# Sums spread between tiles, feed-forward results pair by pair, the hybrid output projection as split products

## What is computed

```python
def swiglu(x, w_in, w_out):
    gate, up = jnp.split(x @ w_in, 2, axis=-1)
    return (jax.nn.silu(gate) * up) @ w_out
...
def sb_rwkv_mixer(hn, w_in, w_out, mu, w0, w2, a0, a2, g2, k_k, k_a, r_k, ln_w, ln_b):
...
    o_a = stick_breaking_attention(hd(qa), hd(ka), hd(va)).reshape(b, s, SB_WIDTH)
    o_b = rwkv7_time_mix(rw, mu, w0, w2, a0, a2, g2, k_k, k_a, r_k, ln_w, ln_b)
    return jnp.concatenate([o_a, o_b.astype(o_a.dtype)], axis=-1) @ w_out
...
        h = h + mix
        h = h + conv_glu(rmsnorm(h, ffn_norm[i]), ffn_w_in[i], ffn_conv_w[i], ffn_conv_b[i], ffn_w_out[i])
        e = rmsnorm(p[i] @ ple_w_proj[i], ple_norm[i])
        gate = jax.nn.sigmoid(rmsnorm(h, ple_gate_norm[i]) @ ple_w_gate[i])
        h = h + gate * e
```

## Time and profile before

| | |
|---|---|
| time, median of 3 runs | 1332.56 us (1331.33 to 1334.46) |
| time of the profiled execution | 1332.49 us |
| its span, first to last instruction | 1330.8 us |
| PE busy | 1305.4 us, 98% |
| DVE busy | 932.6 us, 70% |
| ACT busy | 650.8 us, 49% |
| mean granted PE clock, of the full one | 0.994 |
| fp32 output product of `hyb` (L1136) | 128 records in 28.1 us |

### The profile page before, as it was taken

How to read it: one execution, slowest core, us unless ns; L and a number is a source line. 1 busy time by engine, 2 the same in 40 slices (tenths; PEclk the granted TensorE clock), 3 DMA queues, 4 the chain that set the end, 5 groups by cost and what they waited for, 6 DMA issues and landing times.

```text
span 1330.8 us, 27655 instructions
## 1 busy us (share of the span) xinstructions
PE 1305.4 (98%) x11856; PEld 1261.9 (95%) x11856; DVE 932.6 (70%) x1232; ACT 650.8 (49%) x759; POOL 96.3 (7%) x103
## 2 busy tenths in 40 slices
PE   9999999999999999999999999999999899999998
PEld 8999999998999999999989889999999779999997
DVE  6766666696567666778774457777787776977676
ACT  6444444474345444555624434444375575444445
POOL 0000000141000000003020100000000160000000
PEclk9999999999999999989999999999999999999999
DMA  9555565543355555533420055555544404555540
GB/s 365 192 196 202 201 209 191 190 141 115 133 191 200 204 190 190 189 132 135 169 96 4 1 178 193 199 189 192 199 160 142 158 1 163 197 204 195 189 158 33
DMA packets 34912, 219.16 MB, mean 165 GB/s; under 512 B 4411, under 2 KB 6884, under 8 KB 9612
## 3 DMA queue, kind: packets, MB, share of 16 engines
q1 hardware_dynamic: 32032, 215.62, 45.9%
q10 hardware_dynamic: 2796, 2.31, 0.5%
HBM read 216.72 MB, written 1.06 MB: 164 GB/s over the span
## 4 chain that ended last, share of the span: by engine, by line
PE 92%; DVE 4%; issue 1%; ACT 1%; DMA 1%; POOL 0%; SPq 0%; POOLq 0%; ACTq 0%; DVEq 0%
PE ps L957 47%; PE ps L1003 17%; PE ps L1136 2%; PE ps L920 2%; PE ps L1118 2%; PE ps L900 2%; PE ps L1634 2%; PE ps L1083 2%; PE ps L1281 2%; PE ps L926 1%; PE ps L1676 1%; PE ps L1707 1%; PE ps L1465 1%; DVE arena L2983 1%; PE ps L1474 1%
## 5 line engine op out<-in xcount | busy, mean ns | idle before, releaser
L2604 DVE TENSOR_TENSOR weights_second_parts<-weight_bays,weights_first_parts 128x2048 fp32r<-128x2048 f32 x130 | 296.4, 2288 | 123.5 <-ACT weights_first_parts L1834 123.4
L1834 ACT ACTIVATE weights_first_parts<-weight_bays 128x2048 fp32r<-128x2048 f32 x130 | 248.4, 1914 | 216.4 <-PE ps L957 177.0
L957 PE MATMUL ps<-x_first_part,weights_first_parts 128*128 128x256 f32 x1472 | 195.6, 276 | 0.0
L957 PE MATMUL ps<-x_first_part,weights_second_parts 128*128 128x256 f32 x1472 | 194.5, 275 | 0.0
L957 PE MATMUL ps<-x_second_part,weights_first_parts 128*128 128x256 f32 x1472 | 194.4, 275 | 0.0
L957 PEld LDWEIGHTS ps<-x_first_part,weights_first_parts 128*128 128x128 f32 x1472 | 179.1, 192 | 0.6 <-issue 0.6
L957 PEld LDWEIGHTS ps<-x_first_part,weights_second_parts 128*128 128x128 f32 x1472 | 179.1, 192 | 0.2 <-DVE weights_second_parts L2604 0.2
L957 PEld LDWEIGHTS ps<-x_second_part,weights_first_parts 128*128 128x128 f32 x1472 | 179.2, 192 | 0.0
L1003 PE MATMUL ps<-hidden_first_part,weights_first_parts 128*128 128x256 f32 x704 | 136.3, 275 | 0.0
L1003 PE MATMUL ps<-hidden_second_part,weights_first_parts 128*128 128x256 f32 x704 | 131.5, 275 | 0.0
L1003 PE MATMUL ps<-hidden_first_part,weights_second_parts 128*128 128x256 f32 x704 | 131.5, 275 | 0.0
(11 more groups left out here) (478 smaller groups left out, 2334.2 us busy)
## 6 DMA issues: line engine op xcount, KB each, us to landing
weight_bays<-in_conv_in SPq DMA_DIRECT2D x44, 1024.0 KB, 4.7
weight_bays<-in_ffn_in SPq DMA_DIRECT2D x42, 1024.0 KB, 4.8
weight_bays<-in_ffn_out SPq DMA_DIRECT2D x22, 1024.0 KB, 4.8
weight_bays<-in_conv_out SPq DMA_DIRECT2D x22, 1024.0 KB, 4.8
weight_bays<-in_mix_in SPq DMA_DIRECT2D x19, 1024.0 KB, 4.9
weight_bays<-in_hyb_in SPq DMA_DIRECT2D x13, 1024.0 KB, 4.9
weight_bays<-in_ple_gate SPq DMA_DIRECT2D x12, 1024.0 KB, 4.7
weight_bays<-in_mix_out SPq DMA_DIRECT2D x4, 1024.0 KB, 5.0
```

Of the source, the lines that this page charges most:

```text
L957: mm = nc.tensor.matmul(dst, w[:, k, j * P:j * P + width], x[:, k], start=(n + k == 0), stop=(n == 2 and k == KD - 1))
L1834: nc.scalar.activation(hi, raw, ACT.Copy).then_inc(*w_hi_ready.inc(f, g, kind, of - g))
L2604: v.tensor_tensor(lo, raw, hi, ALU.subtract).then_inc(*w_lo_d.inc(f, g, kind, of - g))
```

## The change

It has three parts, and some that follow from them.

- The sums of squares for the norm behind a `ple` stage are no longer made in one piece at the head of the next stage. Pair 0 is added inside `ple`, ahead of the last gate tile, pairs 1 and 2 at the head of the next stage, pair 3 behind the `embed` of pair 0. In `mix1`, `embed` of pair 1 moves behind the sums. In a `ple` stage DVE adds all four pairs to `h` before it makes second parts of x. DVE's second part of `mix1`'s chunk 1 is made ahead of the norm's factors.
- In a feed-forward's last group the three products are made for two tiles at a time, so that pairs are complete one after another.
- The output product of `hyb` is made of 192 products of split parts in place of 64 products of float32 values. ACT and DVE split its four chunks of weights, the attention outputs (DVE's part of pairs 0 and 1 between levels of the recurrence's inverse) and the recurrence's outputs. `turn_y` moves into the middle of chunk 1.

```diff
@@ -550,7 +550,16 @@
         ysq, _ = carve(at - 3072, 2, 8, 64)
-        oaT = xT[:, 0:4]
+        oa_hi, oa_lo = mixer_hi[:, 0:4], mixer_hi[:, 4:8]
+        ob_hi, _ = carve_split(20480, "recurrent_outputs_first_part", 4, SEQ)
+        ob_lo, _ = carve_split(21504, "recurrent_outputs_second_part", 4, SEQ)
+        hyb_out_hi = [carve_split(n * BAY, f"hybrid_out_first_parts_{n}", BAY)[0] for n in range(4)]
+        def hyb_out_views(n):
+            c = chunks["hyb_out", n] % BAYS
+            return bay[:, c], hyb_out_hi[n][:], bay_lo[:, c]
@@ -870,15 +879,24 @@
-            def add_weighted_squares(n, b):
-                for k in range(KD):
-                    if k % 2 == 0:
-                        pe.wait_ge(*squared.at(n, k // 2))
+            def add_weighted_pair(q, b):
+                for k in (2 * q, 2 * q + 1):
                     for t in range(TT):
                         mm = nc.tensor.matmul(ps[:, b, 2 * t:2 * t + 2], sq[:, k, t * P:(t + 1) * P], gain_pairs[:, k],
                                               start=(k + t == 0), stop=(k == KD - 1), skip_group_check=True)
-                mm.then_inc(*sums_p.inc(n))
+                return mm
+            def add_squares_behind(stage, q):
+                n = key_after(stage)
+                pe.wait_ge(*squared.at(n, q))
+                if n == "hyb":
+                    mm = add_weighted_pair(q, 4)
+                else:
+                    mm = add_pair(sq, q, 4)
+                if q == PAIRS - 1:
+                    mm.then_inc(*sums_p.inc(n))
@@ -1017,14 +1035,16 @@
                         wait_split(pe, (w_lo_d,), f, "out", g, i)
-                        for tile in range(KD):
-                            add(tile, 0, hi, hid_hi)
-                            add(tile, 1, lo, hid_hi)
-                        wait_hidden(pe, hid_lo_ready, f, g, i)
-                        for tile in range(KD):
-                            mm = add(tile, 2, hi, hid_lo)
-                            if tile in (1, 3, 5):
-                                mm.then_inc(*acc_ready.inc(f, tile // 2))
+                        for q in range(PAIRS):
+                            for tile in (2 * q, 2 * q + 1):
+                                add(tile, 0, hi, hid_hi)
+                                add(tile, 1, lo, hid_hi)
+                            if q == 0:
+                                wait_hidden(pe, hid_lo_ready, f, g, i)
+                            for tile in (2 * q, 2 * q + 1):
+                                mm = add(tile, 2, hi, hid_lo)
+                            if q < PAIRS - 1:
+                                mm.then_inc(*acc_ready.inc(f, q))
@@ -1123,33 +1143,16 @@
-            def project_rows(name, srcT, key, at_chunk={}):
...
             def whole_x(n):
                 for q in range(PAIRS):
                     pe.wait_ge(*x_d.at(n, q))
             def mix1():
                 pe.wait_ge(consts_in.sem, 16 * N_CONSTS)
-                embed("ple1", 0, 4, (0, 1))
+                embed("ple1", 0, 4, (0,))
                 add_first_pairs("mix1", 0)
                 add_last_pair("mix1", 0)
-                embed("ple1", 0, 4, (2,))
+                embed("ple1", 0, 4, (1, 2))
@@ -1301,6 +1304,10 @@
                             pe.wait_ge(*ple_d.at(stage, 1))
+                            if stage == "ple1":
+                                pe.wait_ge(*cols_ready.at("block"))
+                            if stage != "ple21":
+                                add_squares_behind(stage, 0)
@@ -1319,12 +1326,13 @@
             def hyb():
-                pe.wait_ge(*rb_ready.at("ple1"))
-                pe.wait_ge(*cols_ready.at("block"))
-                add_weighted_squares("hyb", 4)
-                embed("ple20", 1, 0, (0, 1))
+                add_squares_behind("ple1", 1)
+                add_squares_behind("ple1", 2)
+                embed("ple20", 1, 0, (0,))
+                add_squares_behind("ple1", 3)
+                embed("ple20", 1, 0, (1, 2))
                 spread("hyb", 6, 2)
-                embed("ple20", 1, 0, (2, 3))
+                embed("ple20", 1, 0, (3,))
...
@@ -1598,15 +1606,27 @@
-                def first_rwkv_part():
-                    turn_y()
-                    pe.wait_ge(*sol_d.at("ob", 0))
-                def second_rwkv_part():
-                    pe.wait_ge(*sol_d.at("ob", 1))
-                pe.wait_ge(*stick_a.at("out", 3))
-                project_rows("hyb_out", lambda k: oaT[:, k] if k < 4 else obT[:, k - 4], "hyb", at_chunk={2: first_rwkv_part, 3: second_rwkv_part})
+                for n in range(4):
+                    hi, lo = (t.rearrange("p (a b) -> p a b", a=2) for t in hyb_out_views(n)[1:])
+                    first, second, at = (oa_hi, oa_lo, 2 * n) if n < 2 else (ob_hi, ob_lo, 2 * n - 4)
+                    pe.wait_ge(*w_hi_ready.at("hyb_out", n))
+                    pe.wait_ge(*w_lo_d.at("hyb_out", n))
+                    if n == 0:
+                        pe.wait_ge(*stick_d.at("out", 3))
+                    if n >= 2:
+                        pe.wait_ge(*sol_a.at("ob", n - 2))
+                        pe.wait_ge(*sol_d.at("ob rest", n - 2))
+                    for tile in range(KD):
+                        if (n, tile) == (1, 4):
+                            turn_y()
+                        dst = ps[:, tile // 2, tile % 2 * SEQ:(tile % 2 + 1) * SEQ]
+                        for m, (w, x) in enumerate(((hi, first), (lo, first), (hi, second))):
+                            for j in range(2):
+                                mm = nc.tensor.matmul(dst, w[:, j, tile * P:(tile + 1) * P], in_halves(x[:, at + j]), start=(n + j + m + tile % 2 == 0),
+                                                      stop=(n == 3 and j == 1 and m == 2), skip_group_check=True)
+                        if n == 3 and tile in (1, 3, 5):
+                            mm.then_inc(*acc_ready.inc("hyb", tile // 2))
+                    through(mm, ("hyb_out", n))
...
@@ -2153,7 +2172,7 @@
                     act.wait_ge(*stick_p.at("out", g))
-                    nc.scalar.activation(oaT[:, g], ps[:, STICK_BANK[g], 0:256], ACT.Copy).then_inc(*stick_a.inc("out", g))
+                    nc.scalar.activation(oa_hi[:, g], ps[:, STICK_BANK[g], 0:256], ACT.Copy).then_inc(*stick_a.inc("out", g))
@@ -2201,11 +2220,24 @@
                 stick_weights(3)
+                def first_parts_of_rows(n):
+                    raw, hi, _ = hyb_out_views(n)
+                    wait_weights(act, ("hyb_out", n))
+                    act.wait_ge(*sol_p.at("y", n // 2))
+                    nc.scalar.activation(hi, raw, ACT.Copy).then_inc(*w_hi_ready.inc("hyb_out", n))
                 keep_unknowns(1)
                 stick_keep(2)
+                first_parts_of_rows(0)
+                first_parts_of_rows(1)
                 stick_keep(3)
                 keep_outputs(1)
                 squares_of_outputs(1)
+                first_parts_of_rows(2)
+                first_parts_of_rows(3)
+                for n in range(2):
+                    act.wait_ge(*sol_d.at("ob", n))
+                    nc.scalar.activation(ob_hi[:, 2 * n:2 * n + 2], obT[:, 2 * n:2 * n + 2], ACT.Copy).then_inc(*sol_a.inc("ob", n))
@@ -2505,13 +2537,10 @@
                     update(q, h[:, 2 * q:2 * q + 2]).then_inc(*h_ready.inc(n, q))
-                    if n.startswith("ple"):
-                        if q == 1:
-                            second_parts(n, 0, gain)
-                    elif gain and q:
+                    if gain and q and not n.startswith("ple"):
                         second_parts(n, q - 1, gain)
                 if n.startswith("ple"):
-                    for q in range(1, PAIRS):
+                    for q in range(PAIRS):
...
@@ -3001,13 +3030,24 @@
+                def stick_rest(g):
+                    dve.wait_ge(*stick_a.at("out", g))
+                    v.tensor_tensor(oa_lo[:, g], ps[:, STICK_BANK[g], 0:256], oa_hi[:, g], ALU.subtract).then_inc(*stick_d.inc("out", g))
+                def rest_of_rows(n):
+                    raw, hi, lo = hyb_out_views(n)
+                    dve.wait_ge(*w_hi_ready.at("hyb_out", n))
+                    v.tensor_tensor(lo, raw, hi, ALU.subtract).then_inc(*w_lo_d.inc("hyb_out", n))
                 level(0)
                 stick_softplus(0)
                 level(1)
                 stick_softplus(1)
                 level(2)
                 level(3)
+                stick_rest(0)
                 level(4)
+                stick_rest(1)
@@ -3041,7 +3081,12 @@
                 normed(0)
+                stick_rest(2)
+                rest_of_rows(0)
+                rest_of_rows(1)
+                stick_rest(3)
                 normed(1)
+                rest_of_rows(2)
@@ -3050,6 +3095,11 @@
                     v.tensor_tensor(part, part, ps[:, 6 + n].rearrange("p (a s) -> p a s", a=2), ALU.mult).then_inc(*sol_d.inc("ob", n))
+                for n in range(2):
```

(6 more changed lines are left out.)

31 lines of the change are left out of this document (8 added, 23 removed).

## The result

The changed kernel takes 1324.3 us (median of 4 runs, 1322.65 to 1326.18), the kernel before 1332.7 in the same session: ratio 0.9942, 95% interval 0.993 to 0.9955. That is 8.4 us faster, where 12.85 were forecast. The profiled execution is the slowest of the four: 1326.18 us, span 1324.4. The forecast was 1319.6 us, with a range of 1316.0 to 1325.0. The median lies within that range and 4.7 us above the forecast.

A forecast was written before the change was run, and what follows sets the result against it. The prediction took TensorE's instruction queue to bound the kernel. Its terms -3.6 - 3.0 - 1.5 + 0.65 - 5.4 = -12.85 us took 1332.49 us to 1319.6 us, with a range of 1316.0 to 1325.0.

The forecast's parts named there:

- What bounds the kernel: Whole kernel: TensorE's queue of instructions, busy 1305.4 of 1330.8 us; a change gains by cutting queue, waits or low-clock places.
- Borders: Last feed-forward group into ple, three times: pairs finish earlier, 1.45 us gained at ffn2, 1.1 per conv stage, -3.6 us.
- Heads of `hyb` and `mla`: Heads of hyb and mla: with the sums spread the clock stays up, -3.0 us and -1.5 us.
- Head of `mix1`: mix1's head: embed of pair 1 behind the sums brings a 0.7 us wait, +0.65 us, bounds -0.6 and +2.4.
- falls anew in mix1: Clock rival in mix1's head: wait and sums bring the clock down, 1.7 us, 1321.3 us; all clock cases together 0.2.
- Output of `hyb`: hyb's output product by 192 split products: 7.1 us sooner, part lost at conv0's entry where x is late, -5.4 us.
- the gaps foreseen as 0.5 us between pairs: Sign that the forecast is right: gaps of 0.5 us between pairs at conv0's first features.
- The split products: Rival at hyb's output: products not at the fast rate, 20.6 us more, 1340.2 us; chance 0.03 shared with another new wait.
- The regrouping: Rival at the last groups: regrouping does nothing since x's first part is late anyway, 1323.2 us; chance 0.05.
- keep up at conv0: Rival at conv0's entry: ScalarE and DVE keep up better than walked, 7.1 instead of 5.4 us, 1317.9 us; chance 0.1.

The follow-up runs named there:

- borders_alone: The kernel before with only the last feed-forward group made pair by pair and all additions to h first in the gate stages: 1330.64 us, ratio 0.9982.
- mix1_split: The changed kernel with the 16 sums of mix1's head in two runs of 8, embed of pair 1 between them, the wait kept: 1322.48 us.
- mix1_back: The changed kernel with the order of mix1's head (TensorE and DVE) put back as before: 1320.34 us, ratio 0.9912.
- the entry fix: mix1_back with the third second part of weights behind the additions to h at the entries of ffn2, conv0 and conv1: 1319.04 us, ratio 0.99.

## Why the prediction came out as it did

**What bounds the kernel** was right, and so were the prices read from the earlier trace rows.

**Borders.** Right: 1.0 us at each conv stage against 1.1. For ffn2, `mix_out` begins at 361.09 in the changed kernel and at 358.59 before, so 2.5 - 1.06 = 1.44 us were gained from there to ple1, against 1.45.

**Heads of `hyb` and `mla`.** The clock stayed at 1.00 in both, in every profile with the new order. `mla` gave 1.59 us against 1.5. `hyb` gave 1.06 + 2.10 = 3.16 at x's second parts against 3.0, and then 0.6 were given back in a wait that I had not looked for. PE waits 0.44 us for DVE's fold of the embedding's squares, which comes too late now that PE is ahead. The Trainium skill, page "TensorE: Matmul & The Clock Gate", section "Part 1: The HAM clock gate", read as busy time, had left this step at nothing. The traces don't agree with that reading: PE is busy 20.00 of 20.00 us in `borders_alone` at a clock of 0.91, and 15.19 of 17 us in `mix1_split` at 1.00.

**Head of `mix1`: here the prediction failed.** The step read: "it waits 0.7 us. From there its queue is sums 1.7, ...: +0.65 us", with one fall of the clock as the upper bound (+2.4). The queue was right (+0.78, with a wait of 0.51). The clock was not. The wait and the 16 sums now stand next to each other, and the clock fell here in 5 of 6 profiles, so the head cost 2.5 us, as much as the upper bound and not the term of the sum. I had taken the lack of a fall in `mix1` before as the property of 16 sums, when they had `embed` on both sides and no wait. The rival that names this ("falls anew in mix1", 1321.3 us) had the mechanism, but got too small a chance.

**The clock elsewhere: a term was missing.** The sum took the clock in the untouched parts as fixed by the profile before. It isn't: near 742 us it was up in the profile before and fell in 3 of 6 profiles of the changed kernel, for 3.3 us each. No term or bound of the sum stands for that. The 4.7 us between forecast and median are these: 1.8 for `mix1`'s head (1.7 of clock, 0.1 of queue); 1.5 that I put down to falls near 742 us and in the tail, as the rest of the 4.0 between the changed kernel and `mix1_back` (3.3 in half of the profiles would be 1.65); and 1.4 by which `mix1_back` itself missed its forecast of 1318.95, in which the wait in `hyb` (0.6) and the tail (12.76 us ahead at ple21, 12.2 at the end, 0.6) are the largest. No run of `mix1_back` (5) or of the entry fix (4) has the time of a fall near 742 us. Why such a fall should depend on an order 500 us earlier is open, and it may be chance in so few runs: `borders_alone` has the old order and a short fall there. That the median still lies within the range is in part luck. None of the rivals behind the range is a fall in the middle of `hyb`, and the profiled execution, with both falls, is 1.2 us above its end.

**Output of `hyb`.** Right in size and in its path: 5.16 us against 5.4, a wait of 0.86 against 0.9 before chunk 2, x late at conv0 through DVE's three second parts (the gaps foreseen as 0.5 us between pairs are 0.16 and 0.18 in the brackets of the rows), and 1.5 of the 1.7 us given back there when the queue was cut.

**Other rivals.** The split products ran at the rate of `mix_out`: 72 of them in 774.80 - 766.66 = 8.1 us, 0.113 each. The regrouping did work. ACT and DVE did not keep up at conv0.

## What to carry to other kernels

In this kernel TensorE's busy time does not tell whether it keeps its clock. Before an edit puts a wait beside narrow products, see whether wide ones can stand between them. The same program has several times, 1.7 or 3.3 us apart, by which of its narrow places are hit, so a part is judged by the timeline between two of its instructions at a known clock, and a fall in untouched places belongs into the forecast. When PE is brought forward, the next stall is the written order on the engine that feeds it, where work stands that nobody wants yet.

## What was not expected of the hardware

- The earlier trace rows had the clock fall with PE busy for all of the time, and two variants have it again (20.00 of 20.00 us at 0.83). New is that it falls after a wait as short as 0.51 us, with narrow products next to it, in 5 of 6 profiles. The Trainium skill, page "TensorE: Matmul & The Clock Gate", section "HAM oscillation — how this bites in real kernels", warns of idle gaps from waits for transfers. The waits ahead of the falls here (0.51 and 1.04 us) are for DVE and POOL.
- The same program has falls in different places in different executions: of six profiles of the changed kernel two have both falls, three only the one in `mix1`, one only that in `hyb`. The 23 times of the kernel before in one session group at 1330.4 to 1331.5, 1332.5 to 1333.4 and 1334.1 to 1334.3 us. The mean granted clock of each run goes with them: 0.995 or 0.996 in the first group, 0.994 in the second, 0.992 or 0.993 in the third, and 0.001 of the time is 1.3 us. So the groups differ by their clock. That it is one short fall of 1.7 us more from one to the next fits, but there is one profile of this kernel only.
